# A two-block model on one core: the second mixer's decay cumulative sums are issued one weight unit later, and its four decay matrices three ticks apart in place of one

## What is computed

```python
qkv = silu(causal_dwconv(qkv, conv_w))           # 24 channel blocks of 128
g = -exp(a_log) * softplus(a_logit + dt_bias)    # per token and head
gc = cumsum(g, axis=-1)                          # the "cum" step
diff = gc[..., :, None] - gc[..., None, :]
decay = where(tril, exp(where(tril, diff, 0.0)), 0.0)
lower = where(strict, einsum(k_beta, k) * decay, 0.0)
attn  = where(tril, einsum(q, k) * decay, 0.0)
```

## Time and profile before

| what | value |
|---|---|
| time, median of 3 runs | 1594.82 us (1589.95 to 1594.86) |
| the profiled execution's own time | 1593.63 us |
| its span, first to last instruction | 1591.8 us |
| PE busy | 1538.9 us, 97% of the span |
| PEld busy | 1441.3 us, 91% |
| DVE, ACT, POOL busy | 1027.4, 836.0, 351.7 us |
| mean granted TensorE clock | 0.988 |

### The profile page before, as it was taken

One profiled execution on the slowest core, in us unless ns is written; L12 is line 12 of the kernel. 1 busy time (PEld: TensorE's weight loads), 2 busy tenths in 40 slices (PEclk: granted clock), 3 DMA queues, 4 the chain that ended last, 5 costly groups with the idle time before them and its releaser, 6 DMA issues.

```text
span 1591.8 us, 28579 instructions
## 1 busy us (share of the span) xinstructions
PE 1538.9 (97%) x11138; PEld 1441.3 (91%) x11138; DVE 1027.4 (65%) x1792; ACT 836.0 (53%) x1638; POOL 351.7 (22%) x403
## 2 busy tenths in 40 slices
PE   7799999999988999999999999999999999999998
PEld 6389999999988999999999999999999888888886
DVE  4245467555576875476999976777775555555554
ACT  4155546444446453455444457777775545455454
POOL 1133321000045464231455540011112000000000
PEclk9899999999998999999999999999999999999999
DMA  9632345555533452246455555444445566666664
GB/s 215 223 107 94 107 160 176 174 185 186 172 106 107 130 168 80 94 157 205 136 167 173 172 181 159 138 145 135 146 136 166 190 196 190 194 196 190 195 193 139
DMA packets 76771, 254.20 MB, mean 160 GB/s; under 512 B 11375, under 2 KB 15293, under 8 KB 76509
## 3 DMA queue, kind: packets, MB, share of 16 engines
q1 hardware_dynamic: 76397, 251.71, 49.6%
q0 software_dynamic: 240, 0.66, 0.2%
HBM read 250.23 MB, written 1.84 MB: 158 GB/s over the span
## 4 chain that ended last, share of the span: by engine, by line
PE 79%; DVE 12%; DMA 2%; ACT 2%; POOL 2%; issue 1%; SPq 0%; POOLq 0%; DVEq 0%; ACTq 0%
PE bank L676 78%; DVE wl L1659 4%; DVE big L1659 3%; POOL big L2339 2%; DMA big<-in_w1k 1%; ACT big L1234 1%; DVE big L1662 1%; ACT wh L1234 1%; DVE big L2185 1%; DVE big L2196 1%; DVE big L2192 1%; DVE big L2181 1%; DVE big L2202 1%; DVE big L2189 1%; PE bank L982 0%
## 5 line engine op out<-in xcount | busy, mean ns | idle before, releaser
L1659 DVE TENSOR_TENSOR wl<-raw,wh 128x1024 fp32r<-128x1024 f32 (+4 forms) x459 | 532.3, 1161 | 399.5 <-ACT wh L1234 398.9
L1234 ACT ACTIVATE wh<-raw 128x1024 fp32r<-128x1024 f32 (+1 forms) x459 | 482.3, 1053 | 356.1 <-PE bank L676 338.0
L676 PE MATMUL bank<-gw,wh 128*128 128x256 f32 x3504 | 651.6, 287 | 2.7 <-DVE big L1662 2.7
L676 PEld LDWEIGHTS bank<-gw,wh 128*128 128x128 f32 x3504 | 547.3, 192 | 3.4 <-DVE big L1662 3.1
L676 PE MATMUL bank<-gw,wl 128*128 128x256 f32 x1752 | 497.6, 284 | 6.1 <-POOL wl L2339 5.0
L676 PEld LDWEIGHTS bank<-gw,wl 128*128 128x128 f32 x1752 | 336.6, 192 | 7.8 <-issue 6.3
L676 PE MATMUL bank<-xw,wh 128*128 128x256 f32 x1696 | 323.9, 291 | 10.1 <-ACT wh L1234 7.7
L676 PE MATMUL bank<-wh,xw 128*128 128x512 f32 x1056 | 327.2, 391 | 0.0
L676 PEld LDWEIGHTS bank<-xw,wh 128*128 128x128 f32 x1696 | 267.8, 194 | 18.6 <-ACT wh L1234 8.0
L1234 ACT ACTIVATE big<-bank 128x256 f32<-128x256 f32 (+23 forms) x326 | 118.8, 372 | 260.9 <-PE bank L676 222.7
L2339 POOL TENSOR_TENSOR wl<-raw,wh 128x384 fp32r<-128x384 f32 (+3 forms) x131 | 176.4, 1352 | 343.2 <-ACT wh L1234 343.2
(11 more groups left out here) (136 smaller groups left out, 1108.5 us busy)
## 6 DMA issues: line engine op xcount, KB each, us to landing
raw<-in_wst SPq DMA_DIRECT2D x455, 512.0 KB, 3.7
big<-toeplitz SPq DMA_DIRECT2D x8, 256.0 KB, 14.2
big<-in_w1k SPq DMA_DIRECT2D x4, 512.0 KB, 18.5
big<-in_w1v SPq DMA_DIRECT2D x4, 512.0 KB, 19.5
big<-in_xT SPq DMA_DIRECT2D x4, 256.0 KB, 5.2
raw<-in_wst SPq DMA_DIRECT2D x4, 256.0 KB, 4.9
big<-in_keys SPq DMA_DIRECT2D x1, 1024.0 KB, 5.3
out<-big SPq DMA_DIRECT2D x4, 256.0 KB, 2.4
```

What stands on the lines that cost most here:

```text
L676: return e.matmul(o, a, b, start=first, stop=last, skip_group_check=True)
L1234: return e.activation(o, x, f, **kw)
L1659: return e.tensor_tensor(o, a, b, f)
```

## The change

PE's `cum` step, and DVE's and ACT's reading of it, move one unit on, from slot 122 to slot 123. The four decay groups move from ticks 3, 4, 5, 6 to ticks 8, 11, 14, 17 on PE, DVE's mask stays one tick behind each, and ACT's exponentials stay two ticks behind: from ticks 5, 6, 7, 8 to ticks 10, 13, 16, 19. As `QUADS` is sorted, `("pool", 0)` at tick 10 now stands between decay 0 and decay 1, and the banks of these five follow.

```diff
--- before.py
+++ after.py
@@ -465,7 +465,7 @@
         mgL = steps("merge_lo", range(8))
 
 
-        AT = {("decay", i): 3 + i for i in range(4)}
+        AT = {("decay", i): 8 + 3 * i for i in range(4)}
         AT |= {("pool", g): (10, 22, 35, 49)[g] for g in range(4)}
         for i in range(2):
             AT |= {("sums", i): 21 + 16 * i, ("kd", i): 31 + 16 * i}
@@ -1049,7 +1049,7 @@
                     for tile in range(2):
                         z = e.transpose(b[:, T + 16 * tile:T + 16 * tile + 16], BAT[:, half(tile)], ident[0:16, 0:16])
                     z.then_inc(*baP.sent("tr"))
-                    yield from clock.until(CK, 1)
+                    yield from clock.until(CK + 1, 1)
                     e.wait_ge(*gaG.at("ga"))
                     e.wait_ge(*s_l2.at("inv"))
                     for tile in range(2):
@@ -1466,12 +1466,13 @@
                     act(U2, G2, AF.Abs).then_inc(*gaA.sent("abs"))
                     e.wait_ge(*gaA.at("abs"))
                     act(E2, U2, AF.Exp, scale=-1.0).then_inc(*gaA.sent("small"))
-                    yield from clock.until(CK, 2)
+                    yield from clock.until(CK + 1, 2)
                     e.wait_ge(*gaD.at("ngc"))
                     act(EGC, banks[7][:, 0:16].rearrange("p (a b) -> p a b", b=8), AF.Exp).then_inc(*gaA.sent("egc"))
                     act(ESF, banks[7][:, 16:32].rearrange("p (a b) -> p a b", b=8), AF.Exp).then_inc(*gaA.sent("esf"))
                     for i in range(4):
-                        yield from clock.until(CK + (5 + i) // 4, (5 + i) % 4)
+                        n = AT["decay", i] + 2
+                        yield from clock.until(CK + n // 4, n % 4)
                         e.wait_ge(*dmD.at(i))
                         for j in range(4):
                             h, tile = 2 * i + j // 2, j % 2
```

## The result

The changed kernel takes **1598.09 us** (median of 10 runs, 1595.46 to 1600.01), the kernel before 1594.91 in the same comparison (10 runs): ratio **1.0024**, 95% interval 1.0015 to 1.0033. (A ratio in this document is not the quotient of the two medians given beside it; the two differ by up to 0.0007.) That is 0.24% slower, a difference that is there but lies within 0.3%. Forecast were 1598.0 us and +3.2. The profiled execution took 1598.22 us, with a span of 1596.3.

What follows compares the result with a forecast made beforehand. ACT's queue was taken to set PE's time up to the sums of squares: +3.1 us there and +0.1 behind make +3.2, on the profiled 1593.63 giving 1596.8; the median runs 1.2 higher, so 1598.0 us, range 1593 to 1603.

Steps and rivals of the forecast that it cites:

- PE's stall moves to POOL's low part, 0.7 us: Before the cumulative sums: 0.7 of PE's 1.47 us wait returns as a wait for POOL's share of unit 123.
- ACT's queue sets the time to the sums: Up to the sums of squares: unit 125's `Square` on ACT ends at 509.86 instead of 506.79, +3.1 us.
- Seven loads for three, 5.2 us: ACT's queue, slots 124 to 127: four more table loads at 1.30 us each, 5.2 us.
- A: From start of ACT's split of unit 124 to start of the sums of squares, where the prediction put +3.1 us.
- The rival of loads that don't hide: Loads before decays 0 and 1 add to mask waits: +5.8, 1600.6 us; slower by over 0.3%, chance 0.26 for all such cases.
- the four loads are covered by nothing: The four further loads on ACT are fully exposed; PE waits about 10 us for ACT before the sums of squares.
- A switch costs 1.30: On ACT, the next activation starts 1.30 us after a table load starts, against 2.66 us by the skill's page.
- Behind the sums a constant, +0.1: After the sums of squares start: clock course as before adds +0.1 us, the rest moves by a constant.
- B: From start of the sums of squares to ACT's next table load, at 803.79 us before; prediction there +0.1 us.
- The faster one: Rival: the spread works as lighter bursts on ACT and the kernel wins over 0.3%; chance 0.07.
- first case: Without table switches for the new groups, ACT reaches unit 125's `Square` 4 to 5 us earlier: 1592 to 1594.
- PE's floor: PE unit after unit at full clock, one 0.7 us wait; sums of squares near 497, 10 us and more gained: 1584.

Runs made afterwards that it cites:

- deferred in two parts: Changed kernel with decay groups at PE ticks 16, 17, 24, 25 and their exponentials at ACT ticks 22, 22, 30, 30: 1587.12 us, ratio 0.9964.
- the last experiment: Changed kernel with unit 123's low part made by DVE alone, without a share for POOL: 1597.47 us, ratio 1.0021.
- the run without loads: Changed kernel with Relu in place of Exp in the sixteen decay activations, one table load in place of seven: 1592.68 us, ratio 0.9998.
- the cumulative sums alone: Changed kernel with the decay groups one tick apart (PE ticks 6 to 9), cumulative sums still one unit later: 1589.27 us, ratio 0.9969.
- the spread alone: Kernel before with the decay groups three ticks apart, cumulative sums left in slot 122: 1598.29 us, ratio 1.0027.
- two-and-two: Changed kernel with decays 0 and 1 before the first `Silu`, decays 2 and 3 at PE ticks 16, 17 and ACT tick 22: 1589.71 us, ratio 0.998.
- The two deferred kernels: Changed kernel with all sixteen exponentials in slot 127 behind unit 125's `Square`: 1587.59 us, ratio 0.9966; the other is the kernel deferred in two parts.
- The kernel with 1585.04: Changed kernel with all four decay groups at PE tick 6, sixteen exponentials one tick later before the first `Silu`: 1585.04 us, ratio 0.9952.
- loads added: Kernel before with two tiny exponentials added on ACT in slots 125 and 126, making four more table loads: 1597.9 us, ratio 1.0029.

## Why the prediction was right, point by point

- **PE's stall moves to POOL's low part, 0.7 us.** 0.50 in this profile and in that of the kernel deferred in two parts, 0.71 or 0.72 in five of the others. That it is not on the path to the sums is shown by the last experiment.
- **ACT's queue sets the time to the sums.** Shown. The chain worked out ended at 509.86; measured 510.43, and 0.69 of that is the later start of the split of unit 124, so the working was 0.12 us too long. Its places, less that 0.69: `EGC` forecast 485.72, 485.38; decay 0 491.85, 491.53; decay 1 499.37, 499.05. The second and third came early because the first did: the split of 640 columns on DVE before `NGC`, taken at 1.17 us, was 0.82 from its start to the next.
- **Seven loads for three, 5.2 us.** Their number and their 1.30 us are in the rows after. That they reach the sums is shown twice: by taking six away (A 4.34 less) and by adding four to the kernel before (A 4.67 more). The load hides under its activation's wait for the mask, as assumed; the run without loads shows the waits of 2.40 and 2.41 that lie under them. The rival of loads that don't hide falls with it. But the prediction's sentence that the four loads are covered by nothing is too strong, and against its own working: the new loads before decays 0 and 1 lie under masks that are late without them too, and of the six loads' 7.8 us 3.5 did not reach the sums.
- **A switch costs 1.30.** In the rows after, a load starts as the activation before it ends (within 0.02 us), and the next activation starts 1.29 or 1.30 us after the load does, in all five places where no mask was late. By this the 2.66 us of the Trainium skill's page ScalarE: Activation LUTs, section What ACT_TABLE_LOAD costs, don't hold for this kernel; the load's own 1283 ns do.
- **Behind the sums a constant, +0.1.** Too small: B grew by 0.97. About 0.25 is the clock, back 6.9 us after the start of the sums in place of 6.4. PE's waits near 590 us, where DVE waits for the small matrices from `diag_out`, are 4.1 us in three parts against 3.4 in two; a wait near 520 us is 0.2 shorter, so all waits in B together are 0.5 longer. The last 0.2 stays open. The three-part form is also in four of the other profiles (the cumulative sums alone, the spread alone, the Relu and the two-and-two runs), with A longer and shorter than before; what makes it come was not tried.
- **The rivals.** The faster one had its first case borne out: if the table weren't switched for the new groups, 1592 to 1594, and the Relu run took 1592.68. Its second case was PE's floor, with the sums near 497 us at full clock, 1584. The two deferred kernels have such sums (498.60 and 496.61) and took 1587.59 and 1587.12, as PE waits behind them. The kernel with 1585.04 has its sums at 503.42, so that it comes near 1584 is not that mechanism.

The sum of 3.2 against a measured difference of 3.2 between the medians is luck in its last digit: A was forecast 0.1 too long, B 0.9 too short, A + B grew by 3.9, and the medians of the kernel before moved by 1.3 us from one comparison to the next.

## What to carry to other kernels

Count an engine's table loads as part of its queue when you move an activation: the cost of a step is not only what it lasts but what stands on either side of it. Four groups spread evenly are worse than one block if each meets another function's table; the block did best by its median where the table is already in, here between the last exponential of the gates and the first `Silu`. And look for where the wait goes: the one that the edit removed was 1.47 us, but what its removal was worth, 3.4 us at the sums with close groups and 1.1 with spread ones, was set by ACT's queue.

## What the runs showed that I had not expected

- The stretch behind the sums decides as much as the one before. PE's waits in B and the time in which the clock was at 0.50, both read in windows of 1 us, account for most of the differences in B, if a microsecond at 0.50 is put at half a microsecond (an estimate: around 505 us in the kernel before three matmuls take 0.64 us, at the full clock 0.36, so it is a little under half):

| kernel | A, us | B, us | PE idle in B, us | clock at 0.50 in B, us |
|---|---|---|---|---|
| before | 25.83 | 296.85 | 6.3 | 6.4 |
| changed | 28.78 | 297.82 | 6.8 | 6.9 |
| cumulative sums alone | 22.44 | 297.73 | 6.8 | 6.6 |
| spread alone | 29.90 | 299.54 | 6.3 | 12.3 |
| Relu | 24.44 | 299.47 | 6.3 | 12.1 |
| loads added | 30.50 | 296.74 | 5.6 | 8.2 |
| ahead of `Silu` | 21.73 | 293.70 | 4.8 | 3.4 |
| deferred | 17.05 | 301.27 | 9.6 | 10.2 |
| deferred in two | 15.89 | 300.65 | 9.1 | 6.8 |
| two and two | 19.40 | 301.37 | 8.9 | 10.2 |
| no POOL share | 28.80 | 298.10 | 6.1 | 9.7 |

  The kernel with the exponentials ahead of `Silu` has an A only 0.7 us shorter than the one with the close groups, but its B is 4.0 shorter: 2.0 by PE's waits and about 1.6 by the clock.
- The size of PE's last wait does not tell what the clock does. PE came to the sums from waits of 1.51, 0.65 and 1.29 us with the clock at 1.00 in the kernel ahead of `Silu`; 1.39 and 0.65 us in the run without POOL's share, and the 1.47 us of the kernel before, were followed by 0.50. Where four loads were added, the clock stayed at 1.00 behind the wait of 2.40 us before unit 127 and fell at 509.3 us, in the next one; in the kernel before it fell behind a wait of the same length. And PE's wait of 2.24 or 2.25 us between 587 and 600 us, which every kernel has, is followed by some 3.4 us at 0.50 in six of the eleven profiles (spread alone, Relu, both deferred, two and two, no POOL share) and by none in five. What decides between them was not tried, and as A and B are of one execution each, up to 1.7 us of a B hang on it.
- What an added load costs depends on where it stands. Of the six in the changed kernel that the Relu run took away, 4.34 of 7.8 us reached the sums, as the others lay under waits for masks; of the two pairs put between `Silu` steps, with their exponentials, 4.67 of 5.6 us did; and in the kernel deferred in two parts two more loads than in the deferred one cost nothing that could be measured.
